# A hybrid decoder step on one core: another order of the q, k and v projections, a triangular inversion moved ahead, and a closing sum shared between VectorE and TensorE

## The reference, cut to what matters

```
h = rmsnorm(x);  proj = h @ w_in          # columns: q k v (512 each), z, a, b, u, gate_a, gate_b
q, k, v = silu(causal_conv4(qkv));  q, k = l2norm(q), l2norm(k)
# gated delta rule in chunks of 64 tokens, 8 heads of 64:
decay = exp(gc_i - gc_j) on i >= j        # gc: running sum of g within the chunk
sol = (I + strict_lower(beta k k^T decay))^-1 [beta v, beta k exp(gc)]
scan over 16 chunks:  v_new, o, state
# S5 branch, sigmoid-gated merge, w_o, residual
x = x + moe(rmsnorm(x))                   # 32 experts of 256, two per token
y = rmsnorm(x) * norm_final_w
```

## Time and profile before

| | us |
|---|---|
| median of 3 runs | 1688.06 (1687.43 to 1692.92) |
| the profiled execution's own time | 1691.89 |
| its span, first to last instruction | 1690.2 |
| TensorE busy | 1515.9 (90%) |
| VectorE busy | 737.2 (44%) |
| ScalarE busy | 396.8 (23%) |
| GpSimd busy | 207.9 (12%) |

### The profile page before, as it was taken

The page is one execution under the profiler, slowest core; times in us unless marked ns, Lnnn a source line. Parts: engine busy times, 40 slices in busy tenths (PEclk is TensorE's granted clock), DMA queues, the critical chain, the costliest instruction groups (busy, mean ns, idle before and its releaser), DMA issues.

```text
span 1690.2 us, 16119 instructions
## 1 busy us (share of the span) xinstructions
PE 1515.9 (90%) x6083; PEld 947.4 (56%) x6083; DVE 737.2 (44%) x1295; ACT 396.8 (23%) x639; POOL 207.9 (12%) x224
## 2 busy tenths in 40 slices
PE   8999999989998999699999599999939999999960
PEld 6676666546656656356989466555424444444420
DVE  4667865023253332885785333245432221112118
ACT  3211101116575483231211500011111111111103
POOL 0000100000000000354277000000110000000014
PEclk9999999999999999789899799999969999999985
DMA  5274864414311113224101712132378999999937
GB/s 160 78 126 125 247 206 106 144 52 116 88 52 39 35 31 110 63 63 143 58 1 29 305 57 74 65 114 111 122 268 290 362 374 373 363 368 376 365 126 282
DMA packets 226021, 273.25 MB, mean 162 GB/s; under 512 B 62420, under 2 KB 158024, under 8 KB 225680
## 3 DMA queue, kind: packets, MB, share of 16 engines
q1 hardware_dynamic: 198388, 203.54, 38.3%
q10 hardware_dynamic: 18140, 34.48, 5.4%
q0 software_dynamic: 9408, 34.08, 5.2%
HBM read 188.83 MB, written 83.24 MB: 161 GB/s over the span
## 4 chain that ended last, share of the span: by engine, by line
PE 75%; DVE 8%; ACT 7%; issue 4%; DMA 2%; POOL 2%; ACTq 0%; POOLq 0%; DVEq 0%
PE P L677 23%; PE P L1117 12%; PE P L1068 7%; PE P L1026 7%; PE P L1101 6%; PE P L834 2%; PE P L858 2%; POOL arena L587 2%; PE P L1088 2%; DVE arena L1407 1%; PE P L703 1%; PE P L809 1%; DMA arena<-y_d,arena 1%; DMA x_d<-arena 1%; PE P L692 1%
## 5 line engine op out<-in xcount | busy, mean ns | idle before, releaser
L677 PE MATMUL P<-arena 128*128 128x352 f32 (+1 forms) x1728 | 537.6, 467 | 0.1
L677 PEld LDWEIGHTS P<-arena 128*128 128x128 f32 (+1 forms) x1728 | 325.5, 192 | 186.6 <-issue 27.6
L1117 PE MATMUL P<-arena 128*128 128x512 f32 x512 | 227.1, 597 | 0.8 <-ACT arena L2146 0.8
L1117 PEld LDWEIGHTS P<-arena 128*128 128x128 f32 x512 | 95.6, 192 | 109.5 <-issue 109.5
L1068 PE MATMUL P<-arena 128*128 128x512 f32 (+1 forms) x288 | 128.9, 597 | 1.9 <-DVEq L1565 1.9
L1026 PE MATMUL P<-arena 128*128 128x352 f32 x384 | 115.8, 465 | 8.6 <-DVE arena L1551 8.6
L1709 DVE COPY arena<-P 128x512 f32<-128x512 f32 x32 | 22.1, 691 | 220.3 <-PE P L1088 220.3
L1101 PE MATMUL P<-arena 128*128 128x512 f32 x256 | 115.3, 593 | 0.9 <-DVE arena L1743 0.9
L1026 PEld LDWEIGHTS P<-arena 128*128 128x128 f32 x384 | 74.0, 193 | 50.9 <-issue 11.1
L587 POOL TENSOR_TENSOR arena<-arena,N 64x256 f32<-64x256 f32 x96 | 79.3, 826 | 50.0 <-ACT arena L2081 26.9
L1068 PEld LDWEIGHTS P<-arena 128*128 128x128 f32 (+1 forms) x288 | 50.2, 181 | 62.3 <-issue 59.7
(11 more groups left out here) (393 smaller groups left out, 1877.0 us busy)
## 6 DMA issues: line engine op xcount, KB each, us to landing
arena<-in_w_expert_up_dram SPq DMA_DIRECT2D x32, 2048.0 KB, 13.6
arena<-in_w_expert_down_dram SPq DMA_DIRECT2D x32, 1024.0 KB, 7.9
arena<-in_w_in_dram SPq DMA_DIRECT2D x36, 512.0 KB, 4.2
x_d<-zero SPq DMA_DIRECT2D x4, 4096.0 KB, 20.1
arena<-x_d POOLq DMA_DIRECT2D x32, 512.0 KB, 6.1
y_d<-arena ACTq DMA_DIRECT2D x32, 512.0 KB, 7.9
gate_d<-arena ACTq DMA_DIRECT2D x16, 528.0 KB, 4.4
arena<-gate_d SPq DMA_DIRECT2D x16, 528.0 KB, 4.5
```

Of the source, the lines that this page charges most:

```text
L677: m = pe.matmul(P[0:p, b + j, 0:TBK], w[:, k, 0:p], hT[:, k, TBK * j:TBK * j + TBK], start=f, stop=l)
L1117: m = pe.matmul(P[:, i % 2, :], xgT[i % 2][:, k, :], WU[i % NWE][:, k, :], start=k == 0, stop=k == KD - 1)
```

## The change

Six edits. (1) `JOBS`: q, k, v of pair 0, then q, k of pairs 1 to 3, then v of pairs 1 to 3; the counts follow from the list. The small transposes and the norm's sum of job n-1 come after group 6 only for a q behind a v, after group 5 for a k and for the first q, and else after group 7. A q's `samples` come after group 4 and no longer 2. (2) VectorE's inversion is cut by `invert(lo, hi)`. The prelude (L1472 to L1475) and steps 1 to 11 come at step 30, before VectorE's copies for the last v; steps 12 to 14 before `decays(0)`, and the other three `decays` before steps 21, 26 and 30. (3) The L906 matmuls stand inside jobs 31 to 34, after groups 0 and 2. (4) SyncE loads TP before the weights of job 31. (5) The tail takes the 32-token tile first. Of the nine positions the odd ones (four full tiles) are summed on TensorE: the identity times x1 and two diagonal matrices DG times the gathered rows, accumulated in two PSUM banks. VectorE makes DG during expert tile 6. Gathers go five tiles ahead, outputs have four buffers. (6) TensorE waits at the end of the expert tiles until the last result has been copied out.

```diff
-        JOBS += [("ab", 0)] + [(kind, hp) for hp in range(HP) for kind in "qkv"]
+        JOBS += [("ab", 0)] + [(kind, 0) for kind in "qkv"] + [(kind, hp) for hp in range(1, HP) for kind in "qk"]
+        JOBS += [("v", hp) for hp in range(1, HP)]
...
+        ORDER = [TT_ - 1] + list(range(TT_ - 1))
+        def summed_by_pe(p):
+            return p % 2 == 1
+        def bank_sum(p):
+            return P[:, 2 * (p // 2):2 * (p // 2) + 2, :]
...
-                if i >= 3:
-                    pool.wait_ge(s_acc, i - 2)
+                if p >= GDEPTH and summed_by_pe(p - GDEPTH):
+                    pool.wait_ge(s_job, N_JOBS + (p - GDEPTH) // 2 + 1)
+                elif p >= GDEPTH:
+                    pool.wait_ge(s_acc, (p - GDEPTH) // 2 + 1)
...
-                        if k == (5 if kind == "v" else 2):
+                        if k == {"q": 4, "k": 2, "v": 5}[kind]:
                             samples(m)
...
-                    if post1(m) and k == {"q": 6, "k": 5, "v": 7}[JOBS[m][0]]:
+                    if post1(m) and k == (6 if JOBS[m - 1][0] == "v" and JOBS[m][0] == "q" else
+                                          5 if JOBS[m][0] == "k" or m == AB + 1 else 7):
...
-                if hp < HP:
-                    for q in range(2):
+                def decay_rows(k):
+                    if hp < HP and k in (0, 2):
+                        q = k // 2
                         pe.matmul(bank6()[:, :], head_sel[:, hp, :], gc_row[0:H, 512 * q:512 * q + 512], start=True,
                                   stop=True).then_inc(s_6, 1)
-                job(n)
+                job(n, decay_rows)
...
+                pe.wait_ge(s_yoa, hi)
+                pe.wait_ge(s_yov, hi)
...
+            pe.wait_ge(s_mix, 2)
+            for p, i in enumerate(ORDER):
+                if not summed_by_pe(p):
+                    continue
+                for o in range(2):
+                    pe.matmul(bank_sum(p)[:, o, :], ident, x1[:, i, 512 * o:512 * o + 512], start=True, stop=False)
+                pe.wait_ge(s_yg5[p % GDEPTH], GATHERED[p % GDEPTH] + 32 * (p // GDEPTH + 1))
+                for j in range(2):
+                    for o in range(2):
+                        m = pe.matmul(bank_sum(p)[:, o, :], DG[:, 2 * (p // 2) + j, :], yg[2 * i + j][:, 512 * o:512 * o + 512],
+                                      start=False, stop=j == 1)
+                m.then_inc(s_job, 1)
...
             for n in QSTEPS:
                 m = n - 1
+                if n == N_JOBS_QKV + 1:
+                    invert(1, 12)
...
+            invert(12, 15)
             decays(0)
...
+            invert(15, 21)
+            decays(1)
+            invert(21, 26)
+            decays(2)
+            invert(26, 30)
+            decays(3)
+            invert(30, HC)
             dve.sem_inc(s_inv, 1)
...
+                    if i == 6:
+                        for p in range(1, TT_, 2):
+                            for j in range(2):
+                                m = dve.tensor_scalar(DG[:, 2 * (p // 2) + j, :], ident, w12[j][:, ORDER[p]:ORDER[p] + 1], None,
+                                                      ALU.mult)
+                        m.then_inc(s_mix, 1)
...
+            for p in range(0, TT_, 2):
+                combine(p)
+                if p > 0:
+                    normed(p - 1)
+                normed(p)
...
-            for n in range(N_JOBS_QKV, N_JOBS_QKV + 3):
+            for n in range(N_JOBS_QKV, N_JOBS_QKV + 2):
                 weights(n)
-
             for sm in s_kk:
                 sp.wait_ge(sm, sent[sm])
             sp.dma_start(TP.rearrange("p i j -> p (i j)"), kk_d.rearrange("a b c i j -> (a b c) (i j)")).then_inc(s_tp, 16)
+            weights(N_JOBS_QKV + 2)
```

More of the change, by code:

```diff
@@ L261, in hybrid_step @@
         h2 = [at(q + 4384 + i * D, D) for i in range(2)]
-        yout = [at(q + 6432 + i * D, D) for i in range(2)]
-        junk = yout[0]
+        yout = [at(q + 4384 + i * D, D) for i in range(4)]
+        DG = h2T[0]
+        junk = yout[2]
         WF = at(q + 8480, D)
@@ L428, in hybrid_step @@
         s_wf = sem("s_wf")
+        s_out4 = s_yst + [s_wo, s_wf]
+        STORED = (0, 0, 16, 16)
+        GDEPTH = 5
+        s_yg5 = s_yg + s_h2d
+        GATHERED = [0, 0, 0] + [32 * ((TT_ + 1 - b) // 2) for b in range(2)]
         s_hat = sem("s_hat")
@@ L481, in rows @@
             return min(128, NT - 128 * i)
+        ORDER = [TT_ - 1] + list(range(TT_ - 1))
[3 more added lines that the diff above has]
+            return P[:, 2 * (p // 2):2 * (p // 2) + 2, :]
         w_view = w_in[0].rearrange("(k p) n -> p k n", p=128)
         def QK_COUNT(m):
[L486 removed]
+            return sum(kind != "v" for kind, _ in JOBS[AB + 1:m + 1])
         def KZ_COUNT(m):
[L490 removed]
+            return sum(kind != "q" for kind, _ in JOBS[AB + 1:m + 1])
         n7_scan = N7_X + N7_Y + 1 + 12 + sum({"q": 1 + 1, "k": 1 + 2 + 2 + 1, "v": 1 + 2 + 1}[k] for k, _ in
@@ L1396, in _, with invert @@
             dve.wait_ge(s_ab, 4)
+            def invert(lo, hi):
+                if lo == 1:
+                    dve.wait_ge(s_tp, 16)
+                    dve.tensor_tensor(NA, NA, TP, ALU.mult).then_inc(s_na, 1)
+                    dve.wait_ge(s_na, 1)
+                    link(dve.memset(TP, 0.0))
+                    link(dve.memset(TP.rearrange("p i j -> p (i j)")[:, 0:C * C:C + 1], 1.0))
+                for i in range(lo, hi):
+                    pv = PR[:, 0:2 * i * i].rearrange("p (s j k) -> p s j k", s=2, k=i)
+                    tv = TPb[:, :, 0:i * C].rearrange("p s (j k) -> p s j k", k=C)
+                    link(dve.tensor_tensor(pv, tv[:, :, :, 0:i],
+                                           NAb[:, :, i * C:i * C + i].unsqueeze(2).broadcast_to([128, 2, i, i]), ALU.mult))
+                    link(dve.tensor_reduce(tv[:, :, :, i], pv, AX, ALU.add))
             for n in QSTEPS:
                 m = n - 1
+                if n == N_JOBS_QKV + 1:
+                    invert(1, 12)
                 if post1(m):
@@ L1757, in combine, with normed @@
                                          ALU.add).then_inc(s_acc, 1)
-            combine(0)
-            for i in range(TT_):
+            def normed(p):
+                i = ORDER[p]
                 n = rows(i)
[L1762 to L1766, removed]
+                a = 4 * (p % 2)
+                dve.wait_ge(s_sqf, 2 * (p + 1))
                 link(dve.reciprocal(st[0:n, a + 3:a + 4], st[0:n, a + 2:a + 3]))
-                if i >= 2:
-                    dve.wait_ge(s_yst[i % 2], 16 * (i // 2))
-                dve.scalar_tensor_tensor(yout[i % 2][0:n], o, st[0:n, a + 3:a + 4], WF[0:n, :], ALU.mult,
+                if p >= 4:
+                    dve.wait_ge(s_out4[p % 4], STORED[p % 4] + 16 * (p // 4))
+                o = bank_sum(p).rearrange("p a b -> p (a b)") if summed_by_pe(p) else x1[0:n, i, :]
+                dve.scalar_tensor_tensor(yout[p % 4][0:n], o, st[0:n, a + 3:a + 4], WF[0:n, :], ALU.mult,
                                          ALU.mult).then_inc(s_yout, 1)
+            for p in range(0, TT_, 2):
[3 more added lines that the diff above has]
+                normed(p)
         @block.scalar
@@ L2173, in _ @@
             expert_tiles(act, run)
-            for i in range(TT_):
+            for p, i in enumerate(ORDER):
                 n = rows(i)
[L2177 to L2182, removed]
+                a = 4 * (p % 2)
+                if summed_by_pe(p):
+                    act.wait_ge(s_job, N_JOBS + p // 2 + 1)
+                    o = bank_sum(p).rearrange("p a b -> p (a b)")
+                else:
+                    act.wait_ge(s_acc, p // 2 + 1)
+                    o = x1[0:n, i, :]
+                if p >= 2:
+                    act.wait_ge(s_yout, p - 1)
+                act.activation(JF[0:n, :], o, ACT.Square, accum_out=st[0:n, a:a + 1]).then_inc(s_sqf, 1)
+                act.wait_ge(s_sqf, 2 * p + 1)
                 act.activation(st[0:n, a + 2:a + 3], st[0:n, a:a + 1], ACT.Sqrt, scale=1.0 / D,
@@ L2408, in _ @@
             expert_tiles(sp, run)
-            for i in range(TT_):
-                sp.wait_ge(s_yout, i + 1)
+            for p, i in enumerate(ORDER):
+                sp.wait_ge(s_yout, p + 1)
                 dst = y_p[0, 128 * i:128 * i + 128, :] if i < 8 else y_s.rearrange("b t d -> (b t) d")
-                sp.dma_start(dst, yout[i % 2][0:rows(i), :]).then_inc(s_yst[i % 2], 16)
-            for b in range(2):
-                sp.wait_ge(s_yst[b], 16 * ((TT_ + 1 - b) // 2))
+                sp.dma_start(dst, yout[p % 4][0:rows(i), :]).then_inc(s_out4[p % 4], 16)
+            for b in range(4):
+                sp.wait_ge(s_out4[b], STORED[b] + 16 * ((TT_ + 3 - b) // 4))
             for sm in s_cvo:
```

22 lines of the change are left out of this document (5 added, 17 removed).

## The result

The changed kernel takes **1678.65 us** (median of 5 runs, 1672.2 to 1680.46); the kernel before, run beside it, takes 1692.92 (1687.43 to 1693.87). The ratio is 0.9915, 95% interval 0.9896 to 0.9934: 14.3 us faster, where 21.9 was forecast, and 1678.65 lies just above the range that ended at 1677. The forecast of 1666 started from the earlier median of the kernel before, 1688.06; from 1692.92 the same sum gives 1671. So of the 12.6 us by which it was missed, 4.9 are the starting point and 7.6 the change itself. The profiled execution of the changed kernel is its quickest one: span 1670.5, own time 1672.20, mean granted clock 0.969, while its other four have 0.963 to 0.966.

The account below looks back on a forecast made before the run. TensorE, carrying 75% of the chain of waits, was taken as the bound. Projections +6.5, gate jobs -24.4 and tail -4 sum to -21.9 us, from the median 1688.06 to 1666 us, range 1653 to 1677.

Parts of the forecast that it names:

- The sum of the tail: Tail after the expert tiles: DMA at 334 GB/s sets the pace, 55.9 us falls to 52, so -4 us.
- Rival (c): Tail: TensorE's sums stay at 1.2 GHz and become the bound, tail +8, total 1678 us; chance 0.1.
- The gate jobs: Stretch from projections to `blocks`: VectorE's head start cuts TensorE's waits, 127.0 us becomes 102.6, so -24.4.
- The projections: Projections of q, k and v: waits removed and added by the new order sum to +6.5 us.
- wait of step 24: Projections, step 24: TensorE's 4.4 us wait for VectorE's copies for a v goes; with its clock loss, -6.
- Ln behind a q, twice: Projections, steps 23 and 25: TensorE idles 3.6 us for ScalarE's Ln in a q's norm, twice, +7.2.
- Exp of NA: Projections, step 23: ScalarE's Exp needs its own table load and delays a bank copy beyond its slack, +3.7 us.
- step 30: Projections, step 30: inversion steps 1 to 11 delay VectorE's copies for v3; TensorE waits 1.6 us, taken as +2.
- q's `samples` two groups later: Projections: `samples` after group 4 bring ScalarE's Silu up to 0.5 us later in each step, +1 us.
- clock, net of step 24's: Projections: lower clock after the new Ln waits costs 0 to 6 us, taken as +1, less step 24's clock loss.
- rival (b): Waits only move: Ln and Exp drop the clock, projections +13, gates 112 us, total 1682 us; chance 0.13.
- (d): Slower: with the inversion before VectorE's last v copies, a late TP load stops TensorE in step 30; chance 0.02.

Follow-up runs that it names:

- e9: Kernel before, own job order, with new tail, L906 inside jobs 31 to 34, inversion recut but all behind the projections, L1421 one step later: 1679.65 us, ratio 0.9936.
- e5: Changed kernel with a q's `samples` back after group 2: 1666.88 us, ratio 0.9861 to the kernel before.
- e6: Changed kernel with the Exp of NA and VectorE's block around it four steps later: 1672.58 us, ratio 0.9900 to the kernel before.
- e7: Changed kernel with the norm of a q behind a k earlier (sum after group 5, Ln and Exp before the product copies): 1666.81 us, ratio 0.9858.
- e1: Changed kernel run again with no edit: 1678.36 us, ratio 0.9938 to the kernel before.
- e2: Kernel before with the new tail alone (tile order, sums on TensorE, five gathers ahead, four output buffers): 1685.57 us, ratio 0.9966.
- e11: Changed kernel with all nine tail tiles summed on VectorE; order, gather depth and buffers kept: 1680.67 us, ratio 0.9940 to the kernel before.
- e8: Changed kernel with the edits of e5, e6 and e7 together: 1657.78 us, ratio 0.9810 to the kernel before.

## Why the prediction was right and wrong

**The sum of the tail** was on the careful side: -6.7 instead of -4. It was worked out at the 334 GB/s of the earlier trace rows. Now the gathers are issued back to back, 18 in 24 us (34 before), and from 1635 to 1661 us the DMA engines moved 389 GB/s on average, against 315 from 1650 to 1682 before. The highest slices are no higher than before (420 against 419); the rate is held for longer. First and last gather on GpSimd, and the DMA row from 1620 to 1670 us (GB/s in 40 equal slices):

```profile
1627.58 0.92 POOL L661 DMA_INDIRECT arena<-y_d,arena  x1 [46.38 <-issue]
...
1650.52 0.94 POOL L661 DMA_INDIRECT arena<-y_d,arena  x1 [0.30 <-issue]
```
```profile
GB/s 0 0 279 167 0 7 13 105 118 134 292 246 390 367 351 387 387 324 370 390 400 354 357 406 410 419 393 400 400 419 419 420 419 400 102 3 0 285 288 265
```

Rival (c), TensorE as the tail's bound at 1.2 GHz, didn't come. Only the first four matmuls, behind 13.85 us of idle time, ran at the lower clock; the eight behind them took 3.77 us against 3.60 later on:

```profile
1635.15 3.78 PE L1161 MATMUL P<-arena,shift_id 128*128 128x512 f32 x4 [13.85 <-issue]
1638.73 3.77 PE L1165 MATMUL P<-arena 128*128 128x512 f32 x8
...
1647.48 1.88 PE L1161 MATMUL P<-arena,shift_id 128*128 128x512 f32 x4
1649.20 3.60 PE L1165 MATMUL P<-arena 128*128 128x512 f32 x8
```

**The gate jobs** went as forecast: 103.9 for 102.6, in part by two misses of opposite sign. TensorE was busy for 97.9 us where the terms give 95.4 (a `head_sel` matmul costs 1.05 us and not 0.9, a job 14.5 and not 14.2), and idle for 6.05 where they give 7.2. Counted from the start of step 30 (662.40), VectorE had steps 1 to 11 done at 14.4 (forecast 15), the last one at 93.9 (90), and the inverse's parts reached by TensorE at 122 (118). `decays(2)` and `decays(3)` started 5 us later than I said, but TensorE asked for them later too, by 4 and 8.5 us: waits 3.6 (5), and the lower clock behind them cost 1.7 (12.61 us for 36 matmuls against 10.92) where I allowed 3. The cover of 10 us that the forecast asked for was there; e9 shows what happens without it.

**The projections** are where it failed: +14.2 for +6.5. By its terms:

| term | forecast | measured |
|---|---|---|
| wait of step 24 (its clock, -1.6, is in the last row) | -4.4 | -4.4 |
| transposes for a v's copies | -2.4 | -2.3 |
| Ln behind a q, twice | +7.2 | +6.5 |
| Exp of NA | +3.7 | +3.4 |
| step 30 | +2 | +1.5 |
| q's `samples` two groups later | +1 | +6.8 at the sum, -2.5 at the `samples` |
| clock, net of step 24's | -0.6 | +5.3 (busy time) |

Five terms are within 0.7 us. The measured rows sum to 14.3, 7.8 above the forecast; the clock is 5.9 of that and the `samples` with the sum 3.3, and the other five give 1.4 back. **The step that failed** is "The q's `samples` after group 4 bring ScalarE's Silu [...] up to 0.5 us later in each step", with its "+1", and the clock's "+1" beside it. The first took the move to eat into slack and no more. It moved the copy of the `samples` by two groups, 3.6 us, against 1.5 to 2.3 us of slack (e5), so it had to show as 1.3 to 2.1 us in each of four steps; the slack of 2.28 could have been read before. At the four k's the waits grew by 5.2 us (9.6 against 4.4 of the earlier trace rows); the other 1.6 of the +6.8 is a wait that I missed, of the first q's sum, which the new order asks for after group 5 instead of 6. The second left a span of 0 to 6 and took nearly its lower end, on the ground that ScalarE's chain covers most of a slow stretch and for two waits only; in the profiled execution the lower clock followed the Ln's two waits, the Exp's (for 6.8 us) and one of the `samples`' four, 17.0 us in all, and little of it was covered. e5, e6 and e7 each take away one kind of those waits, and each has 3.6 to 5.3 us less busy time. That this is the clock is shown by the same count of matmuls and by the time at 1.2 GHz, which falls by 6.8 to 10.2 us, about twice as much. Which wait the clock follows isn't forecast by its length, as e5 shows.

So rival (b) was right in one half: its "projections +13" is what happened, by the cause that it names in part (the Ln and the Exp drop the clock) and by one it doesn't name (the `samples`). Its other half, gates at 112, is wrong. (d), the late TP, didn't come: VectorE's prelude began at 661.37, right behind its last copy for v2, with no wait for a load.

**From profile to median.** The pair of profiles differs by 19.7 us: +14.2 -23.1 -6.7, and -4.1 in the rest, of which 2.8 in the first stage, which the change doesn't touch; e1 shows it there too, and e2 to e11 (but e5) don't. That the profile pair comes so near the forecast of 21.9 is luck: the miss in the projections is made up by the tail and by these 4.1. The medians differ by 14.3. The changed kernel's other four executions were 4.6 to 8.3 us longer than the profiled one at a lower mean clock. In which stretches they lost it isn't shown, since one execution of a kernel is profiled; this stays open.

## What to carry to other kernels

Before moving a small operation to a later place to save a wait, look at what stands behind its consumer in that engine's queue, and read the slack of that chain from the timeline: a 0.27 us copy moved by 3.6 us cost some 5 us of waits here over four steps, and 10 us in all with the clock. When waits of 2 to 4 us are added to a busy TensorE, price the matmuls behind some of them at the lower clock as well: here 9.0 us of added waits came with 5.3 us of added busy time. Work that fills gaps of an off-path engine pays when the bound's later waits are for that engine, and then the head start is the gain, not the order of the cuts. Weigh it against what it costs elsewhere: here the order that made it possible lost as much as it won (e9), until e8 repaired it.

## What was not expected of the hardware

Of two waits of the same length, one is followed by the lower clock and one isn't, at the same instruction in two executions of the same program. The changed kernel and then e1:

```profile
489.17 2.04 PE L908 MATMUL P<-arena,head_ones 128*128 128x352 f32 x6 [2.40 <-ACT arena L2089]
```
```profile
489.35 3.70 PE L908 MATMUL P<-arena,head_ones 128*128 128x352 f32 x6 [2.40 <-ACT arena L2089]
```

The wait is 2.40 us in both; the six matmuls take 2.04 us (2.4 GHz) in the one and 3.70 (1.2 GHz) in the other. So at waits of this size the clock is a matter of the execution. Nor does it take a wait of that size: in e8 18 matmuls took 7.09 us behind a wait of 0.84 us, and the next 18 took 5.49. Within each kernel the quicker execution mostly has the higher mean clock (0.969 and 1672.20, 0.963 and 1680.46 in the changed kernel).
